# Row products of the early tile moved out of VectorE's search, with a new order of GpSimd's gathers and scatters

## What is computed

```python
q = (tb @ wq).reshape(PEER_BLOCK, PEER_HEADS, 2, PEER_HALF)
sc = einsum('thpd,pnd->thpn', q, subkeys)
sv, si = top_k(sc, 16)                       # 16 halves of 128 keys
cv, ci = top_k(sv[..., 0, :, None] + sv[..., 1, None, :], 16)
e = i1 * 128 + i2;  g = softmax(cv)
h = einsum('thkd,td->thk', u[e], tb)         # 8 heads x 16 experts for each token
out = einsum('thk,thkd->td', gelu(h) * g, v[e])
```

## Time and profile before

| | us |
|---|---|
| median of 3 runs | 3882.74 |
| lowest to highest | 3880.98 to 3892.97 |
| the profiled execution | 3891.12 |
| its span, first to last instruction | 3889.4 |

### The profile page before, as it was taken

The page is one execution under the profiler, slowest core; times in us unless marked ns, Lnnn a source line. Parts: engine busy times, 40 slices in busy tenths (PEclk is TensorE's granted clock), DMA queues, the critical chain, the costliest instruction groups (busy, mean ns, idle before and its releaser), DMA issues. The chain is left out here.

```text
span 3889.4 us, 45277 instructions
## 1 busy us (share of the span) xinstructions
PE 3322.5 (85%) x15374; PEld 2257.1 (58%) x15398; DVE 2688.9 (69%) x4868; ACT 975.0 (25%) x1832; POOL 1544.3 (40%) x1202
## 2 busy tenths in 40 slices
PE   8898998986888877665757289999999999999998
PEld 7445888974565565544456255555555555555554
DVE  0453878754488566453636888888888888888886
ACT  1452112124122324523655111111111111111112
POOL 0000277720322577578772233333333333333331
PEclk9899999988999988877878699999999999999999
DMA  7897499957888678767586799999999999999996
GB/s 257 339 415 293 168 379 386 384 194 244 333 300 291 184 217 239 171 205 141 140 199 174 248 384 385 381 390 387 388 391 390 392 389 382 390 387 378 384 393 240
DMA packets 488231, 1199.22 MB, mean 308 GB/s; under 512 B 199400, under 2 KB 263320, under 8 KB 425752
## 3 DMA queue, kind: packets, MB, share of 16 engines
q0 software_dynamic: 166768, 674.44, 47.3%
q1 hardware_dynamic: 187760, 502.17, 34.6%
q10 hardware_dynamic: 133568, 20.84, 3.4%
HBM read 1126.54 MB, written 71.83 MB: 308 GB/s over the span
## 5 line engine op out<-in xcount | busy, mean ns | idle before, releaser
L2405 DVE SCALAR_TENSOR_TENSOR d_both<-d_both,k_xn 128x1024 f32<-128x1024 f32 x384 | 460.4, 1222 | 253.4 <-DMA d_both<-peer_uv,d_idx 253.3
L2553 PE MATMUL d_ps<-d_x_high,d_u_high 128*128 128x512 f32 x1024 | 452.4, 442 | 67.4 <-ACT d_u_high L2507 67.4
L2384 POOL DMA_INDIRECT d_both<-peer_uv,d_idx x384 | 451.8, 1176 | 140.2 <-issue 113.1
L1651 POOL DMA_INDIRECT G<-c_cellg,c_cell x256 | 446.4, 1744 | 145.7 <-issue 73.7
L2389 POOL DMA_INDIRECT d_values<-peer_uv,d_idx x128 | 146.5, 1145 | 896.5 <-DVE k_acc L2426 888.6
L2422 DVE SCALAR_TENSOR_TENSOR d_acc<-d_both,d_aw,d_acc 128x1024 f32<-128x1024 f32 x384 | 470.6, 1281 | 4.6
L2571 PE MATMUL d_ps<-k_ring,k_xd 128*128 128x512 f32 x1024 | 451.0, 593 | 0.0
L2571 PE MATMUL d_ps<-d_v,k_xd 128*128 128x512 f32 x1024 | 450.2, 593 | 0.0
L2553 PE MATMUL d_ps<-d_x_low,d_u_high 128*128 128x512 f32 x1024 | 402.0, 393 | 0.0
L1840 DVE SCALAR_TENSOR_TENSOR k_ring<-k_ring,c_xn 128x1024 f32<-128x1024 f32 x128 | 156.1, 1221 | 285.2 <-DMA k_ring<-peer_uv,c_row 284.9
L2571 PEld LDWEIGHTS d_ps<-d_v,k_xd 128*128 128x128 f32 x1024 | 194.7, 190 | 221.8 <-issue 216.9
(11 more groups left out here) (402 smaller groups left out, 5723.6 us busy)
## 6 DMA issues: line engine op xcount, KB each, us to landing
c_chunk<-wq SPq DMA_DIRECT2D x128, 512.0 KB, 6.4
k_ring<-u_blocks SPq DMA_DIRECT2D x128, 512.0 KB, 7.7
s_kc<-sb_kT SPq DMA_DIRECT2D x32, 1024.0 KB, 10.1
s_vc<-sb_v SPq DMA_DIRECT2D x32, 1024.0 KB, 8.3
c_chunk<-w_m SPq DMA_DIRECT2D x64, 512.0 KB, 5.4
k_ring<-v_blocks SPq DMA_DIRECT2D x64, 512.0 KB, 8.6
d_gb<-G SPq DMA_DIRECT2D x64, 512.0 KB, 8.0
d_v<-v_blocks SPq DMA_DIRECT2D x64, 512.0 KB, 9.0
```

Source lines behind the costliest of these rows:

```text
L1651: pool.indirect_dma_start(out=grid, out_offset=bass.IndirectOffsetOnAxis(ap=cell[q][:, s:s + 1], axis=0), in_=cell_g[q][:, s:s + 1], in_of ...
L2384: pool.indirect_dma_start(out=both[par][T][:], out_offset=None, in_=a["peer_uv"], in_offset=bass.IndirectOffsetOnAxis(ap=idx_body[half][:, ...
L2405: last = nc.vector.scalar_tensor_tensor(both[x % 2][T][:, 0:D], both[x % 2][T][:, 0:D], 1.0, xn[:, T], ALU.mult, ALU.mult, accum_out=h[:, ...
L2553: last = nc.tensor.matmul(ps[:, HB + x % 2, :], u_high[:, k], x_part[:, k], start=(k == 0 and n == 0), stop=False)
```

## The change

The dots leave the search. Stage i now has a tuple of six counts: before `gated`, between its two products (`beside`), at each of the six places beside the expert products, after them, after `weigh`, and after `logs(t + 1, 0)` ahead of `residual`. That is 14, 24, 31, 31 and 28 dots for stages 4 to 8.

Rows 0 to 37 (`CALM`) go through six slots 0 to 5, later ones through slots 3 to 5 as before; the one-hot tiles that first use slots 0 to 2, on DVE and ACT, wait for dot 37.

GpSimd's order is 20 rows, 40 scatters, six times 4 rows and 1 scatter, 20 scatters, 31 times 1 row and 1 scatter, 25 scatters, again 31 pairs, 25 scatters, 22 pairs, and the last 56 scatters. The instructions are the same in kind and number.

```diff
@@ -1339,10 +1339,13 @@
     BEFORE, WITHIN, AFTER = {6: 1, 8: 1}, {6: 9, 7: 8, 8: 12, 9: 8}, {6: 3, 8: 3}
     AMONG = {5: 12, 6: 11, 7: 15, 8: 11}
     among = lambda j: AMONG.get(j, 0)
-    BETWEEN, DOTS, DOTS_BESIDE = 29, {4: 16, 5: 20, 6: 19, 7: 21, 8: 10}, {5: 1, 6: 2, 7: 2, 8: 2}
+    DOTS = {4: (0, 2, 0, 3, 3, 6), 5: (0, 2, 0, 10, 5, 7), 6: (3, 3, 2, 5, 2, 6), 7: (3, 3, 2, 5, 2, 6), 8: (5, 4, 2, 7, 0, 0)}
+    CALM = 38
+    early_slot = lambda k: k % 6 if k < CALM else 3 + (k - CALM) % 3
+    early_slots = [early_slot(k) for k in range(P)]
+    early_uses = lambda k: len(range(early_slots[k], REST, RB)) + early_slots[:k + 1].count(early_slots[k])
     NB = 5
     RB = 6
-    EB, EARLY_AT = 3, 3
     QUAD, DEEP, TS = 4, 3, 32
     CHUNKED = HOT * P // QUAD
     CH = TS // QUAD
@@ -1629,35 +1632,50 @@
 
                 def early_rows(n):
 
-                    for k in range(asked[0], min(asked[0] + n, P)):
-                        if k >= EB:
-                            pool.wait_ge(dotted, k - EB + 1)
-                        pool.indirect_dma_start(out=ring[:, EARLY_AT + k % EB], out_offset=None, in_=rows,
-                                                in_offset=bass.IndirectOffsetOnAxis(ap=row0[:, k:k + 1], axis=0)).then_inc(filled[EARLY_AT + k % EB], 16)
-                        asked[0] = k + 1
+                    for k in range(asked[0], asked[0] + n):
+                        s = early_slots[k]
+                        if s in early_slots[:k]:
+                            pool.wait_ge(dotted, k - early_slots[:k][::-1].index(s))
+                        pool.indirect_dma_start(out=ring[:, s], out_offset=None, in_=rows,
+                                                in_offset=bass.IndirectOffsetOnAxis(ap=row0[:, k:k + 1], axis=0)).then_inc(filled[s], 16)
+                    asked[0] += n
 
                 pool.wait_ge(rows_ready, 1)
                 pool.wait_ge(summed, REST)
-                early_rows(DOTS[4] + EB)
-
-                def scatter_head(q, h, rows_after):
-
-                    if h == 0:
-                        pool.wait_ge(dve_r.sem, dve_r.at(SENT[q], "index"))
-                        pool.wait_ge(dve_g.sem, dve_g.at(SENT[q], "g"))
-                    else:
-                        pool.wait_ge(scattered[q], 256 * h)
-                    for s in range(16 * h, 16 * h + 16):
+                early_rows(20)
+
+                sent_on = [0]
+
+                def scatters(n):
+
+                    for at in range(sent_on[0], sent_on[0] + n):
+                        q, s = at // P, at % P
+                        if s == 0:
+                            pool.wait_ge(dve_r.sem, dve_r.at(SENT[q], "index"))
+                            pool.wait_ge(dve_g.sem, dve_g.at(SENT[q], "g"))
+                        elif s % 16 == 0:
+                            pool.wait_ge(scattered[q], 16 * s)
                         pool.indirect_dma_start(out=grid, out_offset=bass.IndirectOffsetOnAxis(ap=cell[q][:, s:s + 1], axis=0),
                                                 in_=cell_g[q][:, s:s + 1], in_offset=None, compute_op=ALU.add).then_inc(scattered[q], 16)
-                        if s % rows_after[0] in rows_after[1]:
-                            early_rows(1)
-
-                for h in range(8):
-                    scatter_head(0, h, (5, (0, 2, 4)))
-                for h in range(8):
-                    scatter_head(1, h, (4, (1,)))
-                early_rows(P)
+                    sent_on[0] += n
+
+                scatters(40)
+                for n in range(6):
+                    early_rows(4)
+                    scatters(1)
+                scatters(20)
+                for n in range(31):
+                    early_rows(1)
+                    scatters(1)
+                scatters(25)
+                for n in range(31):
+                    early_rows(1)
+                    scatters(1)
+                scatters(25)
+                for n in range(22):
+                    early_rows(1)
+                    scatters(1)
+                scatters(2 * P - sent_on[0])
                 for q in range(FIRST_HOT):
                     pool.wait_ge(scattered[q], 256 * 8)
 
@@ -1682,10 +1700,11 @@
                     if name:
                         dve.wait_ge(dve_r.sem, dve_r.at(i, name))
 
-                def gated(i):
+                def gated(i, beside=lambda: None):
                     dve.wait_ge(gate_in, 16 * i)
                     dve.wait_ge(eaten, MERGE_AT[i] + 4)
                     merged(nc.vector.tensor_tensor(gate[:, 1], wide(6), gate[:, 1], ALU.mult))
+                    beside()
                     dve.wait_ge(eaten, MERGE_AT[i] + 8)
                     merged(nc.vector.tensor_tensor(gate[:, 0], wide(2), gate[:, 0], ALU.mult), "gated_a", i)
                     merged(nc.vector.tensor_tensor(gate[:, 0], gate[:, 0], gate[:, 1], ALU.add))
@@ -1835,8 +1854,8 @@
                 def dots(n):
 
                     for k in range(dots_done[0], dots_done[0] + n):
-                        s = EARLY_AT + k % EB
-                        dve.wait_ge(filled[s], 16 * (len(range(s, REST, RB)) + k // EB + 1))
+                        s = early_slots[k]
+                        dve.wait_ge(filled[s], 16 * early_uses(k))
                         nc.vector.scalar_tensor_tensor(ring[:, s], ring[:, s], 1.0, xn0[:], ALU.mult, ALU.mult, accum_out=h0[:, k:k + 1]).then_inc(dotted, 1)
                     dots_done[0] += n
 
@@ -1850,6 +1869,8 @@
                             dve.wait_ge(turned_done, q + 1)
                         if c >= DEEP:
                             dve.wait_ge(spread_done, c - DEEP + 1)
+                        else:
+                            dve.wait_ge(dotted, CALM)
                         nc.vector.tensor_tensor(first[c % DEEP], iota[:, None, :].to_broadcast([P, QUAD, P]),
                                                 turned[:, q, 0, tok:tok + QUAD, None].to_broadcast([P, QUAD, P]), ALU.is_equal).then_inc(firsts, 1)
                     made[0] += n
@@ -1882,8 +1903,6 @@
                             normed(i - 1)
                         if i == 3 and passed[0] in (11, 15, 19, 23):
                             fetch(3)
-                        due = DOTS.get(i, 0)
-                        dots(due * passed[0] // BETWEEN - due * (passed[0] - 1) // BETWEEN)
 
                     between()
                     halves_best(i - 2, between)
@@ -1892,7 +1911,9 @@
                         dve.wait_ge(act_e, 3)
                         dve.wait_ge(gf_in, 16)
                         nc.vector.scalar_tensor_tensor(acc[:], acc[:], fsmall[:, 2:3], gf[:], ALU.mult, ALU.mult).then_inc(dve_e, 1)
-                    gated(i)
+                    dealt = DOTS.get(i, (0,) * 6)
+                    dots(dealt[0])
+                    gated(i, lambda: dots(dealt[1]))
                     one_hots(BEFORE.get(i, 0))
                     left = [WITHIN.get(i, 0)]
 
@@ -1900,15 +1921,18 @@
                         k = min(2, left[0])
                         left[0] -= k
                         one_hots(k)
-                        dots(DOTS_BESIDE.get(i, 0))
+                        dots(dealt[2])
 
                     experts_of(i - 2, beside_products)
+                    dots(dealt[3])
                     weigh(i - 2)
+                    dots(dealt[4])
                     one_hots(AFTER.get(i, 0))
                     if i == 3:
                         fetch(REST - fetches[0])
                     if i < NT - 1:
                         logs(t + 1, 0)
+                        dots(dealt[5])
                         residual(i)
                 residual(NT - 1)
                 normed(NT - 1)
@@ -1959,6 +1983,8 @@
                             act.wait_ge(turned_done, q + 1)
                         if c >= DEEP:
                             act.wait_ge(spread_done, c - DEEP + 1)
+                        else:
+                            act.wait_ge(dotted, CALM)
                         for k in range(QUAD):
                             last = nc.scalar.activation(second[c % DEEP][:, k], iota[:], ACT.Abs, scale=-1.0, bias=turned[:, q, 1, tok + k:tok + k + 1])
                         last.then_inc(distances, 1)
```

## The result

The changed kernel is slower: 3901.39 us median of 17 runs beside 3889.96 us for the kernel before in as many, a ratio of 1.0035 (95% interval 1.0021 to 1.005). Forecast were 3857 us against 3882.7, faster. The profiled execution has a span of 3906.0 us, 16.6 more than before. Of these, 8.3 lie in `decide`, which ends at 2199.8 instead of 2191.5; the other 8.3 lie in `dense` (1706.2 against 1697.9), whose code is the same. The start of `decide` scatters too: `residual(4)`, which ends stage 4, stands between 1270.4 and 1293.0 us in the seven profiled kernels that have the changed places for the dots, though they run nearly the same code up to there.

The account below looks back on a forecast made before the run. The prediction took `decide` to be bound by GpSimd and DVE holding each other up; its stage sums put the border at 2165 instead of 2191.2, 26 us off the 3882.7 median: 3857 us, range 3830 to 3880.

Parts of the forecast that it names:

- The count: Stages 6 to 8: with three slots row k waits for dot k - 3, so searches block GpSimd at rows 41, 72, 103.
- stage 7's search: DVE's search without dots in stage 7: 60 us chosen, ends 44 and 85, most of 30.8 us waits for PE going.
- Stage 4: End of stage 4 moves little, PE being busy 91.77 of 105.80 us: 1290 instead of 1291.9.
- Stage 5: 40 scatters at 2.21 us, then rows 20 to 37 with 4 scatters: ends at 1419, against 1432.4 before.
- The searches of stages 6 and 8: DVE's searches without dots: 52 us in stage 6 (ends 41 and 62), 60 in stage 8 (49 and 70).
- The price of a scatter in a block: Beside an idle DVE in stages 6 to 8: 2.03 us with issue and evenly spread landing waits (1.86 + 0.17).
- The pairs: One gather and one scatter in stages 6 to 8: 3.7 us; 88.8 for 24, 77.7 for 21 in stage 8.
- The tail: After stage 8 GpSimd has 57 scatters, 127.5 us, and about 3 for landing: ends last, at 2165; DVE at 2152.
- The rule on the shared access: Scatters beside dots contend for SBUF; at 2.45 + 0.30 us in 75 pairs the sum would be 53 us more.
- (c): Rival, stages 6 to 8: PE and ACT hold the searches, 272 us instead of 172; 74 us slower, 3957; chance 0.14.
- (d): Rival, bursts of stages 6 to 8: DVE's pauses pass to GpSimd, 27 us, so no difference, 3884; chance 0.12.
- two bounds 83 us apart: The three searches of stages 6 to 8 in sum: floors 134 us, upper ends 217, chosen 172.

Follow-up runs that it names:

- The experiment with the list: The changed kernel with stage 7's one-hot tiles made 1, 1, 1, 1, 1 at blocks 1 to 5 instead of 2, 1, 1, 1: 3880.47 us.
- both edits: The changed kernel with scatter blocks ahead of rows 41, 72 and 103, and stage 7's one-hot tiles one block later: 3755.01 us, 0.9672 of the kernel before.
- two scatters: The kernel with both edits and 254 of its 256 scatters left out, so the grid is incomplete: 3661.86 us in a single run.

## Why the prediction was wrong

The count was right, and the sizes in the sum were not. The step that failed first is stage 7's search, put at 60 us on the ground that its 30.8 us of waits for PE were "itself late through DVE" and would mostly go with the dots; they all stayed, and the search took 78.5 us. Next come the landing waits in the blocks of scatters, spread evenly in the sum, which made the three blocks 15.9 us longer than forecast, and the pairs of stage 8, 6.9 us.

GpSimd blocked by three searches ahead of rows 41, 72 and 103; blocks of scatters that then block DVE; no row waits left in the searches (what the views give there, 0.6, 2.0 and 2.3 us, lies ahead of the last dot before each `residual`); GpSimd last at the border: each of these stands in the trace as forecast, but for the 71.7 us at row 72, where 50 to 60 had been said. With a forecast gain of only 26 us on a chain of some 870, terms that were each off by under 20 turned its sign. The ends of the stages, forecast and measured:

| | forecast | measured | of the stage, forecast and measured |
|---|---|---|---|
| residual(4) | 1290 | 1279.4 | |
| residual(5) | 1419 | 1408.3 | 129, 128.9 |
| residual(6) | 1615 | 1614.8 | 195.7, 206.5 |
| residual(7) | 1833 | 1856.3 | 218.6, 241.5 |
| residual(8) | 2041 | 2073.4 | 207.5, 217.1 |
| border | 2165 | 2199.8 | 124, 126.4 |

- **Stage 4** gave 10.6 us more than the 2 I allowed; part of it is where that execution began (the stage before ended 2.9 us earlier, 1183.2 against 1186.1), the rest is stage 4 itself, 96.2 us for 105.8. I held its search to be PE's; without its 16 dots it took 42.1 us instead of 59.9. But that stage takes 93.9 to 100.3 us in the seven profiled kernels with these places for the dots, so a few us of it are scatter.
- **Stage 5** is exact, terms and all: 40 scatters, 18 rows, and DVE waiting for row 20.
- **The search of stage 7** was the largest miss, 78.5 us for 60. I had the row of 30.8 us and called it "itself late through DVE", which was argued from PE's idle time and not shown. It was a lock step of two lists. The upper end of 85 had it; the chosen value did not. The experiment with the list gives 21 to 26 us; its trace has 24.2 in stage 7 and 26.7 in GpSimd's wait for row 72. That is more than the 18.5 missed because the search without the lock step is 51.9 us and not 60: the 60 was a middle between two ends, and stood for neither case.
- **The searches of stages 6 and 8**, 52.9 and 60.1 us for 52 and 60, were right.
- **The price of a scatter in a block** was mis-sized. From row 41 to row 44 it took 55.2 us for 47, from row 72 to row 75 68.4 for 61.9, from row 103 to row 106 63.1 for 61.9. GpSimd in stages 6 and 7:

```profile
1470.98 1.56 POOL L1658 DMA_INDIRECT G<-c_cellg,c_cell  x1 [0.30 <-issue]
1478.32 2.02 POOL L1658 DMA_INDIRECT G<-c_cellg,c_cell  x1 [5.77 <-DMA G<-c_cellg,c_cell]
...
1506.78 1.56 POOL L1658 DMA_INDIRECT G<-c_cellg,c_cell  x1 [0.30 <-issue]
1514.18 1.56 POOL L1658 DMA_INDIRECT G<-c_cellg,c_cell  x1 [5.84 <-DMA G<-c_cellg,c_cell]
...
1708.44 1.58 POOL L1658 DMA_INDIRECT G<-c_cellg,c_cell  x1 [5.49 <-DMA G<-c_cellg,c_cell]
...
1744.63 1.56 POOL L1658 DMA_INDIRECT G<-c_cellg,c_cell  x1 [5.17 <-DMA G<-c_cellg,c_cell]
```

  The scatters take 1.56 + 0.30 as priced, but the wait at a sixteenth is 5.2 to 5.8 us here; I spread the old 43.5 us evenly, 2.7 for each sixteenth. Two such waits in 21 scatters are 11.6 us where the sum had 3.6. Over all of `decide` they are 57.6 us for 43.5. Why they are longer stays open. It is not only that no row's gather stands between the last scatter and the wait: the one of 5.49 us has row 74 between, and with the blocks three rows earlier the five such waits in the same blocks, with no gather between, were 1.7 to 4.3 us.
- **The pairs** were right in stages 6 and 7: 24 of them took 91.4 and 87.7 us for 88.8. In stage 8 the 21 took 84.6 for 77.7: a gather took 1.25 us and a scatter 1.97 there, against 1.12 and 1.89 in stage 7; why was not looked into.
- **The tail**: 57 scatters and the landing took 134 us for 131.
- **The rule on the shared access** of DVE and GpSimd did not decide. The mean scatter is 1730 ns for 1744; a block beside a waiting DVE runs at 1.56, as the sum had it. In the changed kernel's `decide` the 86 scatters with no DVE instruction beside them took 1.55 to 1.61 us, the 31 beside instructions of the search alone (max, max_index, match_replace) 1.55 to 1.58, and the 48 beside dots alone 1.55 to 2.53, 1.92 on average. That a DVE instruction with two SBUF inputs contends with a GpSimd instruction that reads SBUF, and one with at most one such input does not, outside the modes in which it uses both of its ports, is what the Trainium skill says (SBUF — State Buffer, "Who interferes with whom"). By that rule, the trace agrees.

Of the rivals none came as told. The searches did shorten, so it is not (c), though the result lies on its side; (d) has the size but another cause, since the pairs showed no loss in stages 6 and 7. What I should have done with two bounds 83 us apart (134 and 217 for three searches) and a gain of 26 in the middle is to give "slower" far more than 0.15: the sign turns at 198, and even the 210 from which (c) was to decide was inside my own bounds, with the one row of 30.8 us speaking for it. Forecast 172, the three searches measured 191.5; that alone took 19.5 of the 26. That the measured 3901 us is what (c) gives at my upper ends, 3902, is luck: the searches were 26 us short of those ends, and the blocks and pairs made up for it.

What was not tried: six slots to the end, which would have let the change's order stand as it is. By then slots 0 to 2 belong to the one-hot tiles, so it would need three slots elsewhere; no run shows what it would give.

## What to carry to other kernels

When work is gathered into bursts, the stream that feeds it must be re-cut by the depth of the ring and not by the size of the burst: count, for the last item ahead of each pause of the consumer, which item of the producer it admits, and put the producer's other work right behind that one. Blocks three rows too late in the order cost 119 us here. And where the sum of a change is small against the spread of its least known term, the sign is open; look at that term first, above all when a row in the trace (here four waits of 8 us) can be read as cause or as consequence.

## What the runs showed of the hardware

After the end of its issue, a scatter of 128 four-byte elements took 1.67 to 6.08 us more to land in the changed kernel, in the ten places where GpSimd waited for it with nothing issued between (5.77 and 5.84 us in the rows above). What makes it short or long no run shows.

PE's mean granted clock over a stage was higher where PE stood idle less: 0.78 in stage 7 of the changed kernel with PE busy 140.15 of 241.50 us, 0.88 with both edits and 132.25 of 176.70, 0.92 with two scatters and 131.45 of 163.20. Whether that shortened PE's own work in the stage is not shown: with the blocks three rows earlier it was busy 138.29 us at 0.86, and with the list edit alone 134.36 us at only 0.79.
